# Moving eleven input-projection tiles into the chunked recurrence as plain fp32 matmuls

## The reference, cut to what matters

```python
h = rms_norm(x, norm_in_g)                 # 512 x 1024
p = h @ w_in                               # 1024 x 3596 columns
p_rwkv, p_nsa, p_mem = split(p, ...)       # 2176, 908 and 512 columns
y_rwkv = rwkv7_group(p_rwkv, ...)          # a recurrence over tokens, 8 heads of 64
y_nsa  = nsa_group(p_nsa, ...)             # attention in three branches
y_mem  = memory_group(p_mem, mem_k, mem_v) # attention to 256 memory tokens
x = x + concat(y_rwkv, y_nsa, y_mem) @ w_out
```

## Time and profile before

| what | value |
|---|---|
| runs shown | 2059.31 us median of 3, 2058.52 to 2062.81 |
| the profiled execution's own time | 2064.54 us |
| its span | 2062.4 us |
| mean granted TensorE clock | 0.937 |
| PE busy | 1891.5 us, 92% of the span |
| DVE / ACT / POOL busy | 936.0 / 843.1 / 252.2 us |
| x at the start, 4 DMAs of 512 KB | 8.1 us to landing |
| stage_rwkv_chunks | from 259.5 us to 427.4 us |

### The profile page before, as it was taken

One profiled execution on the slowest core, in us unless ns is written; L12 is line 12 of the kernel. 1 busy time (PEld: TensorE's weight loads), 2 busy tenths in 40 slices (PEclk: granted clock), 3 DMA queues, 4 the chain that ended last, 5 costly groups with the idle time before them and its releaser, 6 DMA issues. The chain is left out here.

```text
span 2062.4 us, 31831 instructions
## 1 busy us (share of the span) xinstructions
PE 1891.5 (92%) x12732; PEld 1529.4 (74%) x12732; DVE 936.0 (45%) x1622; ACT 843.1 (41%) x1361; POOL 252.2 (12%) x209
## 2 busy tenths in 40 slices
PE   6999389969979889989999999999999899999997
PEld 5888088847757657668788888878887778888886
DVE  2343935463355677745333333265554443333333
ACT  4322334434533443543443432275654343444222
POOL 3000223220003220002100000032221020000000
PEclk9999659869989989999999999999999899999998
DMA  4331010010012100002233333222221213232321
GB/s 169 98 92 56 0 43 3 3 45 1 1 42 67 56 26 1 1 21 82 79 95 97 97 95 99 92 77 72 72 74 41 67 57 102 92 102 92 102 92 51
DMA packets 37763, 131.71 MB, mean 64 GB/s; under 512 B 4816, under 2 KB 5136, under 8 KB 37392
## 3 DMA queue, kind: packets, MB, share of 16 engines
q1 hardware_dynamic: 36784, 127.91, 19.9%
q10 hardware_dynamic: 864, 2.17, 0.3%
HBM read 127.17 MB, written 2.10 MB: 63 GB/s over the span
## 5 line engine op out<-in xcount | busy, mean ns | idle before, releaser
L138 DVE TENSOR_TENSOR big_parts<-ring,big_parts 128x1024 fp32r<-128x1024 f32 x164 | 204.8, 1250 | 526.9 <-ACT big_parts L133 526.9
L156 PE MATMUL bank<-h_parts,big_parts 128*128 128x512 f32 x960 | 381.4, 397 | 10.2 <-DVE big_parts L138 6.5
L157 PE MATMUL bank<-y_parts,big_parts 128*128 128x512 f32 x960 | 375.9, 392 | 0.0
L158 PE MATMUL bank<-h_parts,big_parts 128*128 128x512 f32 x960 | 375.6, 391 | 0.0
L133 ACT ACTIVATE big_parts<-ring 128x1024 fp32r<-128x1024 f32 x164 | 173.7, 1061 | 285.6 <-PE bank L158 285.4
L156 PEld LDWEIGHTS bank<-h_parts,big_parts 128*128 128x128 f32 x960 | 181.2, 189 | 56.6 <-issue 12.5
L158 PEld LDWEIGHTS bank<-h_parts,big_parts 128*128 128x128 f32 x960 | 181.5, 189 | 38.5
L157 PEld LDWEIGHTS bank<-y_parts,big_parts 128*128 128x128 f32 x960 | 181.6, 189 | 36.2
L157 PE MATMUL bank<-y_parts,work_parts 128*128 128x512 f32 x456 | 180.2, 395 | 0.0
L138 DVE TENSOR_TENSOR work_parts<-ring,work_parts 128x1024 fp32r<-128x1024 f32 x65 | 79.3, 1223 | 166.8 <-ACT work_parts L133 166.8
L133 ACT ACTIVATE work_parts<-ring 128x1024 fp32r<-128x1024 f32 x65 | 68.7, 1060 | 175.9 <-PE bank L158 175.9
(11 more groups left out here) (404 smaller groups left out, 2999.7 us busy)
## 6 DMA issues: line engine op xcount, KB each, us to landing
ring<-in_wstream SPq DMA_DIRECT2D x229, 512.0 KB, 3.6
x<-in_xt SPq DMA_DIRECT2D x4, 512.0 KB, 8.1
out_t<-x SPq DMA_DIRECT2D x8, 256.0 KB, 2.0
work<-in_memt ACTq DMA_DIRECT2D x1, 1024.0 KB, 15.2
work<-in_cw SPq DMA_DIRECT2D x1, 1024.0 KB, 5.3
cst<-in_cst ACTq DMA_DIRECT2D x1, 704.0 KB, 7.9
cos<-in_reset SPq DMA_DIRECT2D x2, 256.0 KB, 3.3
big<-work SPq DMA_DIRECT2D x4, 128.0 KB, 3.8
```

Source lines behind the costliest of these rows:

```text
L138: dve.tensor_tensor(self.parts[:, self.place_of(n), 1, :, :], self.ring[:, n % RING, :, :], self.parts[:, self.place_of(n), 0, :, :].bitca ...
L156: pe.matmul(out, w[0], x[0], start=start, stop=False, skip_group_check=True)
L157: pe.matmul(out, w[0], x[1], start=False, stop=False, skip_group_check=True)
L158: return pe.matmul(out, w[1], x[0], start=False, stop=stop, skip_group_check=True)
```

## The change

Tiles 17 to 27 leave `stage_in`. The slabs are reordered (17 tiles of the recurrence, 4 memory slabs, then 11 "ns" slabs, then the output projection). In `stage_rwkv_chunks` PE computes tile j (0 to 10) in four parts of two k tiles, one part behind the steps of a level, as plain fp32 matmuls of 128 x 512 straight from the ring slab and from the normed activations: no cast, no split, no parts. Tile j starts at level 9j // 2: the parts stand behind levels 0 to 48 except 8, 17, 26, 35 and 44, 44 parts in all. ACT copies a finished tile to `big` in two halves ahead of its work of level 9j // 2 + 4. The dense tile has PSUM bank 5 for itself, so the steps turn in 5 banks. The normed activations now overwrite `c.x`, since they must live through the stage, and x is loaded a second time in `stage_middle`, behind its tables. In `stage_in` the norm work of the memory tokens is spread over earlier tiles (its sum matmuls, 3.3 us of PE, move from behind tile 15 to behind tile 3), ACT's and DVE's loops over tiles are written out, and the memory tiles use other banks of the same four.

```diff
-IN_TILES, RW_TILES = 28, 17
+RW_TILES, NS_TILES = 17, 11
...
-    for name, n in (("in", IN_TILES), ("mem", 4), ("out", MIX_TILES), ("att", ATT_TILES), ("uq", UQ_TILES // 4),
+    for name, n in (("in", RW_TILES), ("mem", 4), ("ns", NS_TILES), ("out", MIX_TILES), ("att", ATT_TILES), ("uq", UQ_TILES // 4),
...
+    def raw_slab(self, n, k):
+        return self.ring[:, n % RING, k, :]
+    def raw_wait(self, pe, n):
+        pe.wait_ge(self.slab_ready[n % RING], 16 * (n // RING + 1))
...
-    hp = TileParts(c, "in_h", c.h, wkr(c, 15 * T, KT, T), c.yr)
+    hp = TileParts(c, "in_h", c.x, wkr(c, 15 * T, KT, T), c.yr)
...
-            c.load_slabs(sp, 0, n_mem + 4)
+            c.load_slabs(sp, 0, n_mem + 4 + RING)
...
+            for t in range(RW_TILES):
+                c.slab_done_wait(act, n_in + t)
+                c.cast_slab(act, n_in + t + PARTS)
+                act.activation(c.big[:, t, :], c.bank[t % RING][:, :], ACT.Copy, scale=c.omu[:, t:t + 1]).then_inc(scaled, 1)
+                if t == 4:
+                    act.wait_ge(stats, 1)
...
+                if 7 <= t < 7 + KT:
+                    act.wait_ge(memh_ready, t - 6)
+                    mem.scalar(act, t - 7)
...
-                dve.scalar_tensor_tensor(c.h[:, k, :], c.x[:, k, :], vec(c, "norm_in_g", k), c.bank[2][:, :],
+                dve.scalar_tensor_tensor(c.x[:, k, :], c.x[:, k, :], vec(c, "norm_in_g", k), c.bank[2][:, :],
...
-            for t in range(PR_WA + 1, IN_TILES):
-                c.split_slab(dve, n_in + t + PARTS)
-                c.slab_done_wait(dve, n_in + t)
-                dve.tensor_copy(c.big[:, t, :], c.bank[t % RING][:, :]).then_inc(free[t % RING], 1)
...
+DENSE_BANK = 5
+PAIRS = KT // 2
+def first_level(j):
+    return 9 * j // 2
...
+    part_at = {first_level(j) + p: (j, p) for j in range(NS_TILES) for p in range(PAIRS)}
+    out_level = {first_level(j) + PAIRS: j for j in range(NS_TILES)}
...
-            b = sum(1 for k2 in turn if k2[0] not in ("uy", "y")) % 6
+            b = sum(1 for k2 in turn if k2[0] not in ("uy", "y")) % DENSE_BANK
...
-            c.load_slabs(sp, PLAN["out"], PLAN["out"] + RING)
+            c.load_slabs(sp, n_ns + RING, PLAN["out"] + RING)
...
+            def dense(j, p):
+                n = n_ns + j
+                if p == 0:
+                    c.raw_wait(pe, n)
+                    if j:
+                        c.slab_done_wait(pe, n - 1)
+                for k in (2 * p, 2 * p + 1):
+                    mm = pe.matmul(c.bank[DENSE_BANK][:, :], c.raw_slab(n, k), c.x[:, k, :], start=k == 0, stop=k == KT - 1)
+                if p == PAIRS - 1:
+                    mm.then_inc(c.slab_split, 1)
...
+            for lv, level in enumerate(levels):
+                for key in level:
+                    step(key)
+                if lv in part_at:
+                    dense(*part_at[lv])
...
+            def dense_out(j):
+                n, t = n_ns + j, RW_TILES + j
+                c.slab_wait(act, n)
+                act.activation(c.big[:, t, 0:M], c.bank[DENSE_BANK][:, 0:M], ACT.Copy).then_inc(c.slab_cast, 1)
+                act.activation(c.big[:, t, M:T], c.bank[DENSE_BANK][:, M:T], ACT.Copy).then_inc(c.slab_done, 1)
+            for lv, level in enumerate(levels):
+                if lv in out_level:
+                    dense_out(out_level[lv])
+                for key in level:
+                    step(key)
...
+            for i in range(KT // 2):
+                sp.dma_start(c.x[:, 2 * i:2 * i + 2, :], a["xt"][:, 2 * i:2 * i + 2, :]).then_inc(x_loaded, 16)
...
+            sp.wait_ge(x_loaded, 16 * (KT // 2))
```

More of the change, by code:

```diff
@@ L334, in _ @@
             act.wait_ge(omu_ready, 1)
[L335 to L352, removed]
+            for t in range(RW_TILES):
[4 more added lines that the diff above has]
+                    act.wait_ge(stats, 1)
+                    act.activation(root_m, c.bank[6][:, 0:M], ACT.Sqrt, bias=c.eps[:, 0:1], scale=1.0 / D).then_inc(roots, 1)
+                if 7 <= t < 7 + KT:
+                    act.wait_ge(memh_ready, t - 6)
+                    mem.scalar(act, t - 7)
             for j in range(2):
@@ L356, in _ @@
                 c.cast_slab(act, n_mem + PARTS + j)
-                act.activation(c.km[:, j, :], c.bank[j][:, 0:M], ACT.Copy)
+                act.activation(c.km[:, j, :], c.bank[1 + j][:, 0:M], ACT.Copy)
             act.wait_ge(gl_out, 1)
@@ L390, in _ @@
                 tile(u, 0)
[L391 to L400, removed]
+            for k in range(KT):
+                pe.wait_ge(squares, k + 1)
+                mm = pe.matmul(c.bank[6][:, 0:M], con(c, "ones"), squares_m[:, k, :], start=k == 0, stop=k == KT - 1)
+            mm.then_inc(stats, 1)
+            with pe.Fori(1, PR_WA // RING) as i:
+                for u in range(RING):
+                    pe.wait_ge(free[u], i)
+                    tile(u, i)
+            pe.wait_ge(free[0], PR_WA // RING)
+            c.slab_wait(pe, n_in + PR_WA)
+            for k in range(KT):
+                mm = product(pe, c.bank[0][:, :], c.slab_parts(n_in + PR_WA, k), hp.tile(k), k == 0, k == KT - 1)
+            mm.then_inc(c.slab_done, 1)
             for j in range(2):
                 c.slab_wait(pe, n_mem + j)
-                pe.wait_ge(free[j], IN_TILES // RING)
+                pe.wait_ge(free[1 + j], PR_WA // RING)
                 for k in range(KT):
                     mem.wait(pe, k)
-                    mm = product(pe, c.bank[j][:, 0:M], c.slab_parts(n_mem + j, k), mem.tile(k), k == 0, k == KT - 1)
+                    mm = product(pe, c.bank[1 + j][:, 0:M], c.slab_parts(n_mem + j, k), mem.tile(k), k == 0, k == KT - 1)
                 mm.then_inc(c.slab_done, 1)
@@ L412, in _ @@
                     for half in HALVES:
-                        mm = pe.matmul(c.bank[4][half, 12 * q:12 * q + 12], c.h[:, k, q * P:(q + 1) * P][:, half], c.wgl[:, k, :],
+                        mm = pe.matmul(c.bank[4][half, 12 * q:12 * q + 12], c.x[:, k, q * P:(q + 1) * P][:, half], c.wgl[:, k, :],
                                        start=k == 0, stop=k == KT - 1)
@@ L418, in _ @@
                 c.slab_wait(pe, n_mem + 2 + j)
-                pe.wait_ge(free[2 + j], IN_TILES // RING)
+            pe.wait_ge(free[3], PR_WA // RING)
+            pe.wait_ge(free[0], PR_WA // RING + 1)
             for j in range(2):
@@ L449, in _ @@
[L449 to L459, removed]
@@ L604, in rwkv_steps @@
     state = [("uy",), ("sa",), ("y", "st"), ("yt",), ()]
-    steps = []
+    levels = []
     for s in range(NCH + 2):
         for lv in range(5):
+            levels.append([])
             for names, ch in ((first[lv], s), (rest[lv], s - 1), (state[lv], s - 2)):
                 if 0 <= ch < NCH:
-                    steps += [(n, ch) for n in names if not (n == "st" and ch == NCH - 1)]
-    return steps
+                    levels[-1] += [(n, ch) for n in names if not (n == "st" and ch == NCH - 1)]
+    return levels
+DENSE_BANK = 5
+PAIRS = KT // 2
+def first_level(j):
+    return 9 * j // 2
 def stage_rwkv_chunks(c):
@@ L630, in stage_rwkv_chunks @@
     pcb = c.pcb
-    steps = rwkv_steps()
+    levels = rwkv_levels()
+    steps = [key for level in levels for key in level]
+    n_ns = PLAN["ns"]
+    part_at = {first_level(j) + p: (j, p) for j in range(NS_TILES) for p in range(PAIRS)}
+    out_level = {first_level(j) + PAIRS: j for j in range(NS_TILES)}
     by_dve = ("ga", "gb", "ma", "mb", "r2", "r3", "r4", "xt", "v1", "w", "sa", "st", "yt")
@@ L690, in each, with step @@
                 return mm
-            for key in steps:
+            def dense(j, p):
[8 more added lines that the diff above has]
+                    mm.then_inc(c.slab_split, 1)
+            def step(key):
                 name, ch = key
@@ L799, in _, with step @@
             dest = {"p1": "pa", "p1t": "pat", "p2": "pb", "p2t": "pbt", "p3t": "pat", "et": "et", "x": "pa", "x2t": "pbt"}
-            for key in steps:
+            def step(key):
                 name, ch = key
                 if name in by_dve:
-                    continue
+                    return
                 need_made(act, key)
```

37 lines of the change are left out of this document (21 added, 16 removed).

## The result

The changed kernel takes 2043.7 us (median of 6 runs, 2041.77 to 2051.03) against 2058.91 us (6 runs, 2058.1 to 2074.25): a ratio of 0.9919, 95% interval 0.9891 to 0.9948. It is faster by some 15 us, 0.8%, where 25.8 us were forecast; the forecast was 2033.5 us, its range 2022 to 2052.

What follows compares the result with a forecast made beforehand. PE was taken to bound stage_in, and the chunks at a clock of 0.77; stage_middle a DMA, then DVE. Terms -59.8 and +34.0 us gave -25.8, from the 2059.3 median to 2033.5 us, range 2022 to 2052.

Steps and rivals of the forecast that it cites:

- -59.8 for eleven tiles: In stage_in, PE had no idle time, so removing 11 tiles at 5.44 us each saves 59.8 us.
- The clock: In the chunks, the wide matmuls were taken to keep PE at full clock throughout, against 0.77 granted before.
- Rival 1: In the chunks, the clock stays low where it was: +31.7 us, 2091 us; chance 0.10 shared with another slow rival.
- What the parts hide: In the chunks, parts cover PE's waits ahead of L-1, `r4` and `w`, 2.26 us a period; elsewhere paid in full.
- rival 2: In the chunks, the waits are not hidden: +18 us, 2051 us; within a group of cases given 0.18.
- A bank less: In the chunks, steps turning in one PSUM bank fewer cost nothing.
- The sum: Chunks added period by period from steps, parts and remaining waits at full clock: 199.7 us against 168.0 before.
- Changing over: In the chunks, switching between small and wide matmuls: 0.05 us a part, 2.3 in all, bounds 0 and 8.4.
- Period 4: One period of the chunks: 14.7 us of steps plus 8.55 of parts, 23.25 us, changing over left aside.
- stage_middle at 0: stage_middle keeps its 38.6 us: DVE still waits for the tables; at most 1 us lost to the second x load.
- stage_rwkv_prep: The stage between stage_in and the chunks: a difference of 0 forecast.
- The later stages: Everything behind stage_middle, the same code: a difference of 0 forecast.

Runs made afterwards that it cites:

- before_again: The kernel before, unchanged, profiled a second time: span 2046.8 us, chunks 160.9 us.
- five_banks: The kernel before with only the banks in which the steps turn cut from 6 to 5: chunks 168.0 us, stage_middle 40.6 us.
- one_k_tile: The changed kernel with one dense matmul per tile, the other seven k tiles left out: chunks 184.1 us, mean clock 0.76.
- 88 parts: The changed kernel with its 88 dense matmuls in 88 parts of one k tile instead of 44 of two: 2059.75 us, ratio 0.9975.
- 22 and 33 parts: The changed kernel with 22 parts of four k tiles: 2053.56 us; with 33 of 3, 3 and 2, x and last ring slab loaded later: 2044.75 us.
- after_again: The changed kernel itself, unchanged, run again beside the version with 33 parts: 2049.05 us, ratio 0.9938 to the kernel before.

## Why the prediction was right, and where it was off

**-59.8 for eleven tiles: right, and the 60.0 measured agrees with it by luck.** The tiles themselves are as forecast. Two casts of the changed kernel stand 5.44 us apart, so the extra work of ACT and DVE in the tiles cost nothing:

```profile
119.34 1.06 ACT L133 ACTIVATE work_parts<-ring 128x1024 fp32r<-128x1024 f32 x1 [3.50 <-PE bank L166]
124.78 1.06 ACT L133 ACTIVATE work_parts<-ring 128x1024 fp32r<-128x1024 f32 x1 [3.80 <-PE bank L166]
```

But two things beside them cancel. The first profile of before had a stretch of low clock early on that `before_again` had not, and the stage's tail behind the last tile, at full clock before, has a mean of 0.91 in the changed kernel. Windows of before, of `before_again`, and of the tail before:

```profile
30.00:60.00 30.00, 28.13 (x118) 22.78 (x117) 8.59 (x9) 9.99 (x17) 4.98 (x4) 0.94 0.24 70
30.00:60.00 30.00, 28.13 (x124) 22.96 (x124) 9.34 (x10) 9.52 (x15) 4.50 (x4) 1.00 0.24 76
186.00:203.00 17.00, 15.72 (x225) 15.33 (x223) 4.67 (x8) 6.02 (x9) 0.00 (x0) 1.00 0.00 1
```

The tail, from the cast behind the last fp32r tile to the first instruction of prep, takes 18.2 us (124.78 to 142.98) where it took 16.7 (186.28 to 203.02). `before_again` ends the stage at 200.95 and `five_banks` at 201.31: against them 58.0 and 58.3 us went, 1.5 to 1.8 less than forecast.

**The clock: right.** It was the largest choice: 0.99 in place of 0.77, half clock only in the first 6 us. The windows and `one_k_tile` show that the wide matmuls do it, and five more profiles with all 44 or 88 parts have 0.99 too. Rival 1 (2091 us) is out, and the 22 and 33 parts show how near its mechanism is: there the clock falls in places.

**What the parts hide: right.** The period of the changed kernel has no wait left ahead of L-1, `r4` or `w`; rival 2 is out. A bank less is free, as `five_banks` shows. PE's only wait for ACT's copy is 0.23 us, at tile 1. The sum had left 4.6 us of waits in the stage; 2.5 are there.

**Changing over: the term that was mis-sized.** The step was "I take 0.05 each, 2.3, near the row", with bounds of 0 and 8.4. What it cost is 207.6 less the 199.7 of the sum, 7.9 us, 0.18 a part net, nearly the upper bound. By the fits above it is 0.30 for each of the 31 parts behind 64-wide steps, 9.3 us, and nothing for the other 13; the sum's waits were 2.1 us too high, which leaves 0.7 open. Period 4 agrees: three parts of the first kind are 0.90, and it takes 0.92 more than its 23.25. The row chosen, `st` to `p3t`, is a change from 128-wide to 64-wide weights and did hold one side of it: 0.09 of the 1.09 was read as the step's own. It could not show the way from 64-wide weights to a wide part, which is two thirds of the price. This term is 5.6 of the 10 us between forecast and median.

The Trainium skill (TensorE: Matmul & The Clock Gate, Part 2, on LDWEIGHTS) says that a load is pulled ahead of running matmuls when the row groups don't conflict or when it goes to the background weight buffer. The trace agrees within the part, at 0.43, and from a 128-wide step into it, 0.11 ahead. It shows no load pulled ahead from a 64-wide step into a part or out of a part; which of the two conditions fails there no run shows.

**stage_middle at 0: 2.45 us in the profile, not shown to be the change's.** The place was right (DVE waits for the tables, and PE's saved 2.5 us are lost: L1107 takes 3.67 instead of 6.16), but the 7.8 us of the earlier trace rows is the lowest of its kind. The same tables land at 8.7 and 9.8 in two more profiles with the SP stream of before, and at 10.2 to 10.7 in the changed kernel with and without either new transfer. Of the 2.45 us, 1 to 2 are within what the kernel before does by itself. The longer issues of SP stand in nearly all profiles of the changed kernel and in none of before, so a part may well be the change's; their cause stays open.

**stage_rwkv_prep: +0.9, not the change's.** The two profiles differ there in the clock (0.63 and 0.61). `five_banks`, which is the kernel before in this stage, takes 57.3 us there at 0.60, and `after_again` takes 56.5 at 0.63.

**The later stages: -4.75 us, not the change's own.** Windows at the end of the first feed-forward stage, before and then after:

```profile
1340.00:1344.00 4.00, 4.00 (x73) 3.40 (x72) 1.07 (x4) 0.63 (x1) 0.00 (x0) 0.99 0.00 0
1344.00:1348.00 4.00, 4.00 (x15) 3.24 (x15) 2.80 (x5) 2.19 (x3) 0.00 (x0) 0.59 0.02 4
```

```profile
1321.30:1325.30 4.00, 4.00 (x46) 3.21 (x46) 0.69 (x1) 0.12 (x1) 0.00 (x0) 1.00 0.00 0
1325.30:1329.30 4.00, 4.00 (x56) 3.74 (x54) 2.04 (x7) 2.70 (x4) 0.00 (x0) 1.00 0.00 0
```

In the norm that ends the stage, behind a stream of one-column matmuls, the clock falls to half in one execution and stays up in another: eight matmul instructions of 256 columns take 3.68 us and 1.99, and the stage 379.1 and 377.7. `before_again` has 1588.8 us behind `stage_middle`, the kernel with 33 parts 1597.8. Without this share the first profiles differ by 17.1 us, which is near the 15.2 of the medians; the forecast's sum had 25.8.

**One profile of before was taken as the kernel.** Against `before_again` the span falls by 6.2 us only (2046.8 to 2040.6), with 46.7 us more in the chunks instead of 39.6. That execution is the fastest of before on record, and the medians stand; but the runs of both kernels scatter by 9 to 16 us, and the mean clock moves with them: the changed kernel's fastest run (2041.77 us) has 0.957, its slowest (2051.03) 0.952.

## What to carry to other kernels

Work put into the gaps of a chain of small dependent matmuls costs its own time less the gaps, plus what it costs to go from narrow weights to wide ones and back. Here that was 0.30 us for each part between 64-wide steps and nothing behind a 128-wide step, so look for places behind wide steps first, and count the changes as terms of the sum. Such work can pay for itself through the clock: here 75 us of plain fp32 matmuls cost 39.6 us. Half clock fell from some 77 us of the stage (a mean of 0.77 over 168 us) to 6, each worth half at most, and PE's idle time from 17.9 us to 4.0. Fewer and larger parts saved changes here and lost as much or more to the clock and to waits. Profile the kernel before twice before a few microseconds are argued about.

## What the runs showed of the hardware that was not expected

- PE busy 20.00 of 20.00 us with 64 x 64 matmuls and the clock at 0.50, beside 10.94 of 12.00 at 1.00 in the same stage. A share of busy time does not tell the clock.
- A stretch of 128-wide matmuls between 64-wide ones costs 0.30 us beyond its matmuls, whatever its length (1, 2 or 4 k tiles): 0.10 ahead of it, 0.10 in its first matmul, 0.10 at its end. The first wide load starts with its own matmul, not 0.11 ahead of it as behind a 128-wide step, and the first narrow load comes 0.95 us after the last wide one, where wide ones follow at 0.43. Behind a 128-wide step the stretch costs nothing beyond its matmuls (2.81 us against 1.09 + 1.71).
- The clock also falls behind very narrow streams: 64 gate matmuls of 12 columns (the tail of `stage_in`, 0.91 after, 1.00 before) and one-column matmuls (0.59 before, 1.00 after) are followed by half clock in some profiles and not in others.
- The same eight tables land 7.8, 8.7 and 9.8 us after the barrier in three profiles with the same SP stream, and a DMA issue that takes 0.33 to 0.59 us in one of them takes up to 2.5 in the variants of the changed kernel.
